# The last block's down projection in two halves of 256 tokens, and the final norm shared by three engines

## What is computed

```python
def rmsnorm(x, g):
    xf = x.astype(jnp.float32)
    y = xf * lax.rsqrt(jnp.mean(xf * xf, axis=-1, keepdims=True) + EPS)
    return (y * g.astype(jnp.float32)).astype(x.dtype)

def swiglu(h, w1, w3, w2):
    return (jax.nn.silu(h @ w1) * (h @ w3)) @ w2

# end of block(), and of reference()
h = rmsnorm(x, norm_ffn2) * (1.0 + m(7)) + m(6)
x = x + 0.5 * m(8) * swiglu(h, w1_ffn2, w3_ffn2, w2_ffn2)
y = rmsnorm(x, final_norm)
```

## Time and profile before

| | us |
|---|---|
| median of 3 timed runs | 1367.88 |
| lowest, highest | 1333.22, 1456.43 |
| the profiled execution | 1334.19 |
| its span on the slowest core (core 6) | 1332.7 |
| spans of the 8 cores | 1324.1 to 1332.7 |
| PE, DVE, ACT, POOL busy (core 6) | 1260.2, 519.2, 380.0, 179.9 |

### The profile page before, as it was taken

The page is one execution under the profiler, slowest core; times in us unless marked ns, Lnnn a source line. Parts: engine busy times, 40 slices in busy tenths (PEclk is TensorE's granted clock), DMA queues, the critical chain, the costliest instruction groups (busy, mean ns, idle before and its releaser), DMA issues.

```text
span 1332.7 us, 18779 instructions; the slowest of 8 cores (1324.1 to 1332.7 us)
## 1 busy us (share of the span) xinstructions
PE 1260.2 (95%) x6592; PEld 570.7 (43%) x6592; DVE 519.2 (39%) x794; ACT 380.0 (29%) x625; POOL 179.9 (13%) x300
## 2 busy tenths in 40 slices
PE   2699999999998999899999989999999999999996
PEld 1244444444444444344444334444444444444442
DVE  2143243211331345576366645531243212432446
ACT  3354100111001244766435325621100111001343
POOL 3122001000010000123324222310001000000000
PEclk9899999999998999999999989999999999999998
DMA  9985456422569310002412213622313111020223
GB/s 176 224 185 79 80 85 94 76 32 32 91 92 151 97 64 1 1 1 53 76 24 51 86 37 90 110 49 42 59 27 62 34 32 32 0 48 1 61 63 130
DMA packets 33835, 90.93 MB, mean 68 GB/s; under 512 B 3888, under 2 KB 8400, under 8 KB 31568
## 3 DMA queue, kind: packets, MB, share of 16 engines
q0 software_dynamic: 21792, 62.01, 28.8%
q1 hardware_dynamic: 11952, 27.73, 6.4%
HBM read 137.04 MB, written 14.68 MB: 114 GB/s over the span
## 4 chain that ended last, share of the span: by engine, by line
PE 87%; DMA 5%; DVE 3%; issue 2%; ACT 2%; POOL 1%; DVEq 0%; ACTq 0%; SPq 0%; POOLq 0%
PE ps L235 87%; DMA sb_arena<-w_ada 3%; DVE sb_arena L263 2%; ACT sb_arena L248 2%; DMA sb_arena<-x 1%; DVE sb_arena L252 1%; PE ps L239 0%; POOL sb_arena L232 0%; POOL sb_arena L257 0%; ACT L248 0%; DVE sb_arena L730 0%; POOL sb_arena L252 0%; DVEq L141 0%; DVEq L1136 0%; ACTq L141 0%
## 5 line engine op out<-in xcount | busy, mean ns | idle before, releaser
L235 PE MATMUL ps<-sb_arena 128*128 128x512 bf16 (+4 forms) x5792 | 1204.1, 368 | 13.1 <-DVE sb_arena L252 5.4
L235 PEld LDWEIGHTS ps<-sb_arena 128*128 128x128 bf16 (+3 forms) x5792 | 534.9, 98 | 671.1 <-issue 62.2
L248 ACT ACTIVATE sb_arena<-ps 128x512 f32<-128x512 f32 (+3 forms) x272 | 161.1, 600 | 749.5 <-PE ps L235 743.6
L252 DVE TENSOR_TENSOR sb_arena<-sb_arena,ps 128x512 bf16<-128x512 f32 (+1 forms) x208 | 143.0, 688 | 505.3 <-PE ps L235 403.0
L263 DVE SCALAR_TENSOR_TENSOR sb_arena<-ps,sb_der,sb_arena 128x512 f32<-128x512 f32 x192 | 144.1, 751 | 160.7 <-PE ps L235 160.7
L248 ACT ACTIVATE sb_arena<-sb_arena 128x512 bf16<-128x512 f32 (+2 forms) x184 | 115.2, 678 | 39.3 <-DMA sb_arena<-x 17.7
L232 POOL DMA_DIRECT2D sb_arena<-w_ffn x88 | 47.1, 545 | 440.2 <-PE ps L235 410.1
L252 DVE TENSOR_TENSOR sb_arena<-sb_arena 128x512 f32<-128x512 f32 x96 | 64.5, 713 | 22.4 <-ACT sb_arena L248 22.4
L259 POOL TENSOR_SCALAR sb_arena<-sb_arena,sb_der,sb_modT 128x512 bf16<-128x512 f32 x44 | 39.8, 907 | 223.8 <-DVE sb_arena L252 192.7
L235 PE MATMUL ps<-sb_arena,sb_onesB 128*128 128x512 bf16 x144 | 42.4, 406 | 27.2 <-ACT sb_arena L248 25.5
L248 ACT ACTIVATE sb_arena<-sb_arena,sb_modT,sb_der 128x512 bf16<-128x512 f32 x48 | 39.0, 812 | 69.1 <-DVE sb_arena L252 55.5
(11 more groups left out here) (40 smaller groups left out, 157.7 us busy)
## 6 DMA issues: line engine op xcount, KB each, us to landing
sb_arena<-w_ffn POOLq DMA_DIRECT2D x44, 512.0 KB, 7.6
sb_arena<-w_ada POOLq DMA_DIRECT2D x36, 512.0 KB, 9.3
sb_arena<-w_ffn POOLq DMA_DIRECT2D x44, 256.0 KB, 9.9
sb_arena<-x SPq DMA_DIRECT2D x8, 1024.0 KB, 13.4
y<-sb_arena SPq DMA_DIRECT2D x32, 256.0 KB, 3.6
xspill<-sb_arena SPq DMA_DIRECT2D x4, 1024.0 KB, 3.9
sb_arena<-xspill SPq DMA_DIRECT2D x4, 1024.0 KB, 5.9
sb_arena<-w_cv POOLq DMA_DIRECT2D x12, 256.0 KB, 7.9
```

What stands on the lines that cost most here:

```text
L235: return P.add("pe", lambda e: e.matmul(out, lhsT, rhs, start=start, stop=stop), reads=flat(reads), writes=flat(writes))
L248: return P.add("act", lambda e: e.activation(out=out, in_=in_, func=func, **kw), reads=flat(reads), writes=flat(writes))
L252: return P.add(eng, lambda e: e.tensor_tensor(out=out, in0=in0, in1=in1, op=op), reads=flat(reads), writes=flat(writes))
```

## The change

`ffn_last` gets a rate for its ticks in the down part (2 in place of 1) and leaves out the last entry of `seq`; the last block's down part is then written as two halves of 256 tokens by `last_half`, each with products of 256 columns, an STT, a square on ACT, and for d = 1, 3, 5 a scaling by the final norm's gain on ACT in place. It returns the half's stats and eight applications: a tensor-tensor with rstd on POOL for d = 1, 3, 5, an STT on DVE for the others, each with an output DMA of 128 x 256 f32. `split_last` makes tiles for the halves, so that each has dependences of its own. For the first three blocks `final_apply` does odd kc by a scaling on ACT and a tensor-tensor on POOL. The squares and rstd of the halves lie in the region of h (HT), which nothing reads any more.

```diff
-        def ffn_last(F, order, after_down, hooks):
+        def ffn_last(F, order, after_down, hooks, rate=1, stop=0):
...
-            for kind, i in seq:
+            for kind, i in seq[:len(seq) - stop]:
...
                     for d in range(8):
                         F.down(16, 6, d, blk)
-                        tick(1)
+                        tick(rate)
...
         def final_apply(blk):
             def f(kc, r, t_r):
-                stt(xv(kc, blk), xv(kc, blk), vcol(FN + kc), r, ALU.mult, ALU.mult, [t_x[kc][blk], t_vec, t_r], [t_x[kc][blk]])
+                if kc % 2 == 1:
+                    act(xv(kc, blk), xv(kc, blk), AF.Identity, [t_x[kc][blk], t_vec], [t_x[kc][blk]], scale=vcol(FN + kc))
+                    tt("pool", xv(kc, blk), xv(kc, blk), r, ALU.mult, [t_x[kc][blk], t_r], [t_x[kc][blk]])
+                else:
+                    stt(xv(kc, blk), xv(kc, blk), vcol(FN + kc), r, ALU.mult, ALU.mult, [t_x[kc][blk], t_vec, t_r], [t_x[kc][blk]])
                 dma("sp", y_d[kc, :, blk * 512:(blk + 1) * 512], xv(kc, blk), [t_x[kc][blk]], [], "y%d_%d" % (blk, kc))
             return f
...
-        ffn_last(F2, ORD, after2, {})
+        def last_half(blk, hf):
+
+            h0 = hf * 256
+            st = {}
+
+            def squares(d):
+                o = HT + hf * 4 * KB + d * 512
+                st[d] = (bf(o, 256), P.alloc("sqh%d_%d" % (hf, d), o, 512))
+                act(st[d][0], xv(d, blk)[:, h0:h0 + 256], AF.Square, [t_xh[hf][d]], [st[d][1]])
+                if d in PO:
+                    act(xv(d, blk)[:, h0:h0 + 256], xv(d, blk)[:, h0:h0 + 256], AF.Identity, [t_xh[hf][d], t_vec], [t_xh[hf][d]],
+                        scale=vcol(FN + d))
+
+            def stats():
+                for d in range(8):
+                    mm(ps[:, 7, h0:h0 + 256], onesB[:], st[d][0], d == 0, d == 7, [t_ones, st[d][1]], [t_ps[7]])
+                r = f32(HT + (8 + hf) * KB, 256)
+                t_r = P.alloc("rh%d" % hf, HT + (8 + hf) * KB, KB)
+                act(r, ps[:, 7, h0:h0 + 256], AF.Ln, [t_ps[7]], [t_r], scale=1.0 / D, bias=EPS)
+                act(r, r, AF.Exp, [t_r], [t_r], scale=-0.5)
+                st["r"] = (r, t_r)
+
+            def app(d):
+                r, t_r = st["r"]
+                xh = xv(d, blk)[:, h0:h0 + 256]
+                if d in PO:
+                    tt("pool", xh, xh, r, ALU.mult, [t_xh[hf][d], t_r], [t_xh[hf][d]])
+                else:
+                    stt(xh, xh, vcol(FN + d), r, ALU.mult, ALU.mult, [t_xh[hf][d], t_vec, t_r], [t_xh[hf][d]])
+                dma("sp", y_d[d, :, blk * 512 + h0:blk * 512 + h0 + 256], xh, [t_xh[hf][d]], [], "yh%d_%d" % (hf, d))
+
+            PO = (1, 3, 5)
+            for d in range(8):
+                b = 4 + cnt["dn"] % 2
+                cnt["dn"] += 1
+                for i in range(6):
+                    w, t_w = F2.w2[16 + i]
+                    g, t_g = F2.g[(16 + i, blk)]
+                    mm(ps[:, b, 0:256], w[:, d * 128:(d + 1) * 128], g[:, h0:h0 + 256], i == 0, i == 5, [t_w, t_g], [t_ps[b]])
+                xh = xv(d, blk)[:, h0:h0 + 256]
+                stt(xh, ps[:, b, 0:256], der[:, G2 + d:G2 + d + 1], xh, ALU.mult, ALU.add,
+                    [t_ps[b], t_dr["G2"], t_xh[hf][d]], [t_xh[hf][d]])
+                squares(d)
+                tick(2)
+            return [stats] + [(lambda d=d: app(d)) for d in (1, 0, 3, 2, 5, 4, 6, 7)]
...
+        ffn_last(F2, ORD, after2, {}, rate=2, stop=1)
+        split_last(ORD[3])
+        later(None, last_half(ORD[3], 0))
+        tail2 = last_half(ORD[3], 1)
         drain()
+        for f in tail2:
+            f()
```

More of the change, by code:

```diff
@@ new lines, in build_program, with split_last @@
+        t_xh = [[None] * 8 for _ in range(2)]
+        def split_last(blk):
+            for d in range(8):
+                src = t_x[d][blk]
+                for hf in range(2):
+                    t = Tile("xh%d_%d" % (d, hf))
+                    t.writer = src.writer
+                    t.readers = dict(src.readers)
+                    t_xh[hf][d] = t
+        ffn_last(F2, ORD, after2, {}, rate=2, stop=1)
+        split_last(ORD[3])
+        later(None, last_half(ORD[3], 0))
+        tail2 = last_half(ORD[3], 1)
```

## The result

The changed kernel takes 1341.75 us (median of 6 runs, 1340.5 to 1342.83). The kernel before, run beside it, took 1335.22 in the median of 6; three of these are the runs shown ahead of the prediction (1333.22, 1367.88, 1456.43), the later three lie at 1333.92 to 1336.22. The ratio is 1.0055, with a 95% interval of [1.004, 1.007]: slower by half a per cent, some 7.3 us (5.3 to 9.3), and inside the 2% that count as a difference here.

The account below looks back on a forecast made before the run. PE was taken to bind until about 1316 us, then DVE. Last issue 1334.6, landing 1337.1, span end 1337.4: +4.7 on 1332.7, so about 1338.9 from 1334.19; range 1331 to 1344, extended to 1371 for run scatter.

Parts of the forecast that it names:

- The outputs: End of the kernel: 16 issues of 128 KB, 2.5 us to landing, span end 0.3 later at 1337.4.
- three signs of being wrong: Tail: last rstd before 1327, final products under 3 us, or a half product on PE not near 0.108.
- ACT's new order: Third block's squares queue behind the half's first square; they end at 1310.6, and PE stands about 3 us before the stats.
- The first half's rstd: Last block, first half: rstd at 1321.7, after DVE alternates products of 512 with STTs of 256.
- the last rstd: Last block, second half: PE ends at 1327.5, then STT, square, stat, Ln and Exp give rstd at 1330.05.
- the last product: Tail: the last eight products, five on DVE and three on POOL, take 4.0 us, ending at 1334.1.
- The gain (a): Before the down stage: one DVE product fewer ahead of the first down STT, at two places: -0.6 us (0 to -0.7).
- New shapes: Width 256, durations in us: DVE STT 0.48, ACT 0.41, scaling 0.50, POOL product 0.75, PE product 0.108.
- rival 3: PE: a half product costs as much as a whole one (0.216 us), ending 3.7 later, at 1342.6; chance 0.15.
- DVE and POOL in turns: Tail: products with two SBUF inputs alternate, each holding the other up; the last eight take 4.0 us, eight on DVE 3.3.
- rival 1: Tail: DVE and POOL share freely without blocking; +1.5 us, giving 1335.7; chance 0.15.
- Rival 2: The change wins: short wait for squares, free sharing, shorter end; -2.1 us, giving 1332.1; chance 0.15.

Follow-up runs that it names:

- third experiment: Changed kernel with the third block's eight squares put into ACT's queue ahead of the first half (`tick(4)`): 1340.9 us, ratio 1.003.
- tenth experiment: Kernel before with the changed `final_apply` alone, in all four blocks, no halves: no ratio; comparable runs 1343.59 and 1343.73 beside 1337.79.
- sixth experiment: Changed kernel, third block's squares ahead of the first half, second half's products all on DVE (both repairs), 12 output semaphores for 44: 1335.78 us, ratio 1.0001.
- eighth experiment: Kernel before, whole blocks, only reordered: third block's norm earlier, last block's squares one by one behind its STTs: 1334.0 us, ratio 0.9992.
- fourth kernel: Changed kernel with all final-norm products on DVE, no POOL or ACT scalings, halves kept: 1344.67 us, ratio 1.0074.
- eleventh: Reordered whole-block kernel with ACT and POOL only for kc 1, 3, 5 of the third block: 1335.64 us, ratio 0.9983.
- twelfth kernels: Reordered whole-block kernel, POOL for third block's kc 1, 3, 5, DVE's product of d = 6 put off: 1360.12 beside 1359.54, no ratio.
- fifth: Changed kernel, third block's squares ahead of the first half and second half's products all on DVE: 1336.34 us, ratio 1.001.

## Why the prediction was right and wrong

**The step that failed** is the last of "The outputs": "Last issue 1334.6, landing 1337.1, end of the span 0.3 later". The landing came 1.3 earlier than forecast (42.5 behind the anchor, not 43.8), but the end came 4.7 us behind it and not 0.3. POOL's DRAIN was not in the sum. I let the end follow from the outputs because it did so in the kernel before, where POOL had been idle for over 100 us. The change gives POOL work up to the end for the first time, and an engine has a DRAIN to pass before the block can close, 8.1 us on POOL. It was in the trace of before, among the queue's own instructions (12.4 us at 1187.5); I did not ask what the end waits for beside DMA. Shown both ways: one operation of 0.20 us added to the kernel before gives 4.2 us in the trace (first experiment), and taking POOL out of the second half alone takes 3.65 of them back (second). Without the DRAIN the changed kernel would have ended at about 43.8 behind the anchor, against the forecast's 44.1. That is an estimate: SP's last wait, at 43.5, and the 0.3 from there to the end in the second experiment.

**The size and the sign.** Reckoned from the profiled execution, +4.7 was forecast; the two traces give +7.8 and the ratio +7.3. The direction against that execution was right. The amount is short by the 4.4 of the DRAIN, less 1.3 by which the outputs landed before their forecast: two errors that partly cancel. The number written down, 1338.9, reads as a gain beside the median of 1367.88 that stood there; against the 1334.07 that is the median of the four runs compared, it reads as the loss that it is. None of the three signs of being wrong that I named came (the last rstd before 1327, final products under 3 us, a half product far from 0.108): all three look at the way to the last product, not at what follows it.

**ACT's new order** (the squares behind the half's first): right in place and size. Behind the anchor the squares were to end at 17.3 and ended at 17.5; rstd of the third block 20.5 and 20.7; PE goes on at 21.9 and 22.1; PE stood 3 us and 3.0. The third experiment prices it, at 3.4 us.

**The first half's rstd** was forecast at 28.4 and came at 28.3; **the last rstd** 36.7 and 36.2; **the last product** 40.8 and 39.9. The gain (a) ahead of the down part was taken at 0.6 and was 0.35: the third block's last whole STT starts at 10.8 behind the anchor, before at 11.1.

**New shapes.** STT of 256 was 0.478 (0.48 taken), ACT 0.411 (0.41), the scaling 0.507 (0.50), POOL's product of 256 0.72 for the first of each three and 0.90 for the others, beside DVE's products (0.75 taken). Twelve half products on PE take 1.47 with one latency, so about 0.11 each (0.108): rival 3 falls. Its 1342.6 is the number nearest to the measured 1341.75, but that is chance: the half products were as cheap as forecast, and what it lacked was the DRAIN.

**DVE and POOL in turns.** Right in kind, so rival 1 falls; a bit cheaper than reckoned. A DVE product of 512 that meets POOL took 1.37, I had 1.57; the last eight took 3.6 from 1330.49, I had 4.0. Against whole products of POOL on both sides it took 1.745 (tenth experiment). By the Trainium skill (SBUF — State Buffer, "Who interferes with whom") the ports that DVE shares with GpSimd are an exclusive lock. The 1.745 and 1.37 in place of 0.75 agree in kind.

**The outputs.** Issue to landing was at least 1.9 for 128 KB, I had 2.5; here is the tile y of the changed kernel:

```profile
L232 SPq DMA_DIRECT2D y<-sb_arena x40: 332/385/409, 1257.7 to 1334.7; - x40
...
DMA to landing us min/median/max: 1.9/2.6/4.5
```

SP's waits at the end, 44 for 36, weren't in the sum either; they cost 1.0 once POOL was out of the way (sixth experiment).

**Rival 2** (the change wins) was given 0.15 "if PE stands under 3 us in all". It did stand longer. But its other half, an earlier rstd of the third block, may be worth something: without the halves and with the slices placed by hand, the last block's squares among them, the last product comes 2.2 us earlier in the trace (eighth experiment), though the ratio doesn't tell this from none.

**The halves** themselves won nothing: with both repairs and 12 semaphores the kernel with halves stands at the kernel before (1.0001, sixth experiment).

**Open.** Why the fourth kernel is 2.4 to 3.0 later rather than 0.8 is read from its rows (2.4 on DVE, 0.6 on cores whose clock stayed low for longer), not shown by a run that changes one of the two. Why the clock falls on some cores and not on others is not known. Whether the eleventh and twelfth kernels are faster than the eighth was not settled.

## What to carry to other kernels

Before you give a so far idle engine work at the very end, look up what its own closing instruction costs in the trace: here POOL's last operation set the end, even one of 0.20 us, when it ended less than 8.1 us ahead of the last landing; one that ended 9 to 10 us ahead cost nothing. Sharing element-wise work between DVE and POOL relieved DVE here where DVE had something to do that didn't meet POOL's (STT from PSUM); side by side on SBUF the pair was no quicker than DVE alone (3.56 against 3.26 us for the last eight half products, 6.9 against 5.4 for eight whole ones). When background work is fed in by ticks, check what comes to stand ahead of it in each engine's queue: four slices taken one statement earlier were worth 3.4 us.

## What the runs showed of the hardware

- POOL's closing DRAIN ended 8.1 us behind its last computing operation, on all eight cores, be that a tensor-tensor of 512 or 256 columns, one of 8 columns (0.20 us) or a memset of 2 (0.10 us). Behind DMA issues as POOL's last instructions it ended 10.8 to 14.4 us later.
- The granted clock fell to 0.50 for some cores and not for others of the same program, after PE had stood in the waits of the first half. It cost these 1.85 us in the fifth and sixth kernels. With 20 added products of 256 columns all eight stayed at 1.00, in one profiled execution.
- A semaphore wait on SP took about 0.05 us even when it was met: with 44 of them the span ended 1.3 us behind the last landing, with 12 it ended 0.3 behind.
